# Moving two table builds beside the first MLP, 45 modulation columns into the sparse attention, and the first SwiGLU layer into seven-product blocks

## What is computed

```python
def first_block(...):             # one layer
    z = rms_norm(h, g_mix) @ w_in # q, k, v of sparse attention, an RNN, cross attention, gates
    y = gm0 * nsa_mixer(...) + gm1 * (gelu(g_rnn) * rg_lru(...)) + gm2 * cross_attention(...)
    h = h + y @ w_o
    h = h + square(relu(rms_norm(h, g_mlp) @ w_up)) @ w_down     # "the MLP", 1024 -> 4096 -> 1024
    return rms_norm(h, g_final)

def second_block(x, c, ...):      # two layers
    for l in range(2):
        mod = (silu(c) @ mod_w[l] + mod_b[l]).reshape(bsz, 3, 3, 1024)   # scale, shift, gain
        x = post_add(x, swiglu(pre(x, 0), ffn_w_in[l, 0], ffn_w_out[l, 0]), 0, 0.5)
        x = post_add(x, token_mixer(pre(x, 1), ...), 1, 1.0)   # state-space model and attention
        x = post_add(x, swiglu(pre(x, 2), ffn_w_in[l, 1], ffn_w_out[l, 1]), 2, 0.5)
```

## Time and profile before

| | |
|---|---|
| median of 3 runs | 3378.67 us (3377.63 to 3381.85) |
| the profiled execution, its own time | 3385.66 us |
| its span in the profile | 3383.9 us |
| PE busy | 3317.5 us, 98% |
| DVE, ACT, POOL busy | 62%, 43%, 13% |
| mean DMA rate | 118 GB/s |

### The profile page before, as it was taken

The page is one execution under the profiler, slowest core; times in us unless marked ns, Lnnn a source line. Parts: engine busy times, 40 slices in busy tenths (PEclk is TensorE's granted clock), DMA queues, the critical chain, the costliest instruction groups (busy, mean ns, idle before and its releaser), DMA issues.

```text
span 3383.9 us, 45115 instructions
## 1 busy us (share of the span) xinstructions
PE 3317.5 (98%) x18265; PEld 2709.1 (80%) x18273; DVE 2099.3 (62%) x3034; ACT 1439.4 (43%) x2316; POOL 427.6 (13%) x321
## 2 busy tenths in 40 slices
PE   9999999999999999999999999999999999999998
PEld 6755477688888888888768899979998875879998
DVE  5555566578687644565334777777777533367775
ACT  3365465442323332233443454445444245245543
POOL 0100012122232001022002100020001210220001
PEclk9999999999999999999999999999999999999999
DMA  5311543254655234213122132222323331222232
GB/s 195 138 55 60 184 180 142 107 192 180 251 215 197 98 126 153 87 64 136 69 83 98 64 108 98 100 88 94 107 107 110 115 106 44 101 74 100 95 106 75
DMA packets 83711, 398.01 MB, mean 118 GB/s; under 512 B 9136, under 2 KB 20016, under 8 KB 53296
## 3 DMA queue, kind: packets, MB, share of 16 engines
q1 hardware_dynamic: 71088, 370.41, 30.5%
q10 hardware_dynamic: 12416, 24.71, 2.0%
HBM read 374.12 MB, written 20.97 MB: 117 GB/s over the span
## 4 chain that ended last, share of the span: by engine, by line
PE 89%; DVE 6%; ACT 2%; issue 2%; POOL 1%; DMA 0%; SPq 0%; ACTq 0%; DVEq 0%; POOLq 0%
PE pb L817 13%; PE pb L819 13%; PE pb L818 13%; PE pb L1324 6%; PE pb L1323 6%; PE pb L1322 6%; PE pb L1363 3%; PE pb L1364 3%; PE pb L1365 3%; PE pb L718 2%; PE pb L785 2%; PE pb L786 2%; PE pb L1019 1%; PE pb L793 1%; PE pb L720 1%
## 5 line engine op out<-in xcount | busy, mean ns | idle before, releaser
L2453 DVE TENSOR_TENSOR wl<-w,wh 128x2048 fp32r<-128x2048 f32 (+2 forms) x179 | 390.4, 2181 | 439.6 <-ACT wh L1587 439.0
L817 PE MATMUL pb<-XH,wh 128*128 128x512 f32 (+2 forms) x1528 | 611.4, 400 | 2.3 <-DVE wl L2453 1.6
L819 PE MATMUL pb<-XH,wl 128*128 128x512 f32 (+2 forms) x1528 | 597.0, 391 | 0.0
L818 PE MATMUL pb<-XL,wh 128*128 128x512 f32 (+2 forms) x1528 | 596.7, 391 | 0.0
L1587 ACT ACTIVATE wh<-w 128x2048 fp32r<-128x2048 f32 (+2 forms) x179 | 309.6, 1729 | 178.0 <-PE pb L819 88.0
L817 PEld LDWEIGHTS pb<-XH,wh 128*128 128x128 f32 (+2 forms) x1528 | 286.1, 187 | 70.7 <-issue 8.2
L818 PEld LDWEIGHTS pb<-XL,wh 128*128 128x128 f32 (+2 forms) x1528 | 286.2, 187 | 64.1 <-issue 4.6
L819 PEld LDWEIGHTS pb<-XH,wl 128*128 128x128 f32 (+2 forms) x1528 | 285.7, 187 | 63.3
L1983 ACT ACTIVATE wh<-w 128x1024 fp32r<-128x1024 f32 x228 | 191.8, 842 | 91.1 <-DVE w L3012 75.5
L2997 DVE TENSOR_TENSOR wl<-w,wh 128x1024 fp32r<-128x1024 f32 x228 | 217.0, 953 | 13.8 <-ACT wh L1983 13.6
L2440 DVE CUSTOM_DVE_ANT_0 mreg<-mreg,pr 128x1024 f32<-128x1024 f32 x144 | 200.3, 1407 | 37.7 <-DMA mreg<-in_mod_w 37.4
(11 more groups left out here) (650 smaller groups left out, 7531.0 us busy)
## 6 DMA issues: line engine op xcount, KB each, us to landing
mreg<-in_mod_w SPq DMA_DIRECT2D x144, 512.0 KB, 3.5
w<-in_f_wide SPq DMA_DIRECT2D x57, 1024.0 KB, 4.8
w<-in_f_piece SPq DMA_DIRECT2D x48, 512.0 KB, 3.2
w<-in_f_in SPq DMA_DIRECT2D x22, 1024.0 KB, 4.8
w<-in_w_up SPq DMA_DIRECT2D x16, 1024.0 KB, 5.7
w<-in_w_dn SPq DMA_DIRECT2D x16, 1024.0 KB, 5.7
w<-in_m_g SPq DMA_DIRECT2D x16, 1024.0 KB, 4.8
w<-in_f_out SPq DMA_DIRECT2D x16, 768.0 KB, 4.2
```

The lines of the kernel that those rows point to most:

```text
L817: mm(dst, hi[:, cs], xh[:, k, :], start=k == 0, stop=False)
L818: mm(dst, hi[:, cs], xl[:, k, :], start=False, stop=False)
L819: x = mm(dst, lo[:, cs], xh[:, k, :], start=False, stop=fin)
L2453: tt(low[:, 0:s.cols], wslots[b % 3][:, 0:s.cols], h[:, 0:s.cols].bitcast(F32), ALU.subtract).then_inc(*DV.up(("lo", b), ("w_free", b)))
```

## The change

It does four things. All four SwiGLU layers use seven-product blocks, so the plain path is gone. Both table builds run beside the MLP: build 1 and then build 0, each padded to 66 steps, three steps a tile for the first 12 of the 64 tiles and two from there on; both layers' tables are stored to DRAM and loaded back at the end of layers 0 and 2. DVE's order inside a build is changed (the pieces `answers` before `lags`), with a second buffer for the turned weights, and both builds share one work space; build 0 waits for build 1's table store. And the modulation columns are spread anew: two for a block in the projections k, c, q (8 more loads), 21 in the rows half (after each third step) and all 8 of 8 steps in the keys half (64 in place of 48), one in place of two for a block of the MLP, where 12 are left of 57.

```diff
-        self.two_columns = name == "o" or name == ("m", 2) or name[0] in ("up", "dn")
+        self.two_columns = name in ("k", "c", "q", "o") or name == ("m", 2)
 for _n in range(64):
-    NSA_ROWS += [("s", _n)] + [("j", 0)] * (_n % 8 in (1, 4, 6)) + [("c", 0)] * (_n == 57) + [("y", 0)] * (_n == 59)
+    NSA_ROWS += [("s", _n)] + [("m", 0)] * (_n % 3 == 2) + [("j", 0)] * (_n % 8 in (1, 4, 6)) + [("c", 0)] * (_n == 57) + [("y", 0)] * (_n == 59)
...
-    NSA_KEYS += [("m", 0)] * (1 <= _j <= 6) + [("h", 0)] * (_n == 45)
+    NSA_KEYS += [("m", 0)] + [("h", 0)] * (_n == 45)
-WIDE_FFN = (1, 2, 3)
+WIDE_FFN = (0, 1, 2, 3)
-BUILD_A, BUILD_K, BUILD_B, BUILD_T = 16, 33, 34, 45
-BUILD_STORE = 59
+BUILD_A, BUILD_B, BUILD_K, BUILD_T = 18, 32, 43, 49
+BUILD_STORE, BUILD_END = 60, 66
+def some_steps(steps, tile):
+    for _ in range(3 if tile < 12 else 2):
+        next(steps, None)
...
                 if s.name == "qx":
-                    ahead(s.b[0] + 4)
-                    for n in range(48):
+                    for n in range(5):
+                        ahead(s.b[0] + n)
+                        for _ in range(4):
+                            mod()
+                    for n in range(1 + 64):
                         mod()
...
             def mlp():
-                extra = ssm_build(1)
+                extra, tile = itertools.chain(padded(ssm_build(1)), padded(ssm_build(0))), itertools.count()
...
             def ffn(l, f):
-                extra = ssm_build(0) if i == 0 else iter(())
...
+                run(st_of[("in", i, 0)], XH, XL, xw(r))
+                third_block(i)
+                for what, n in WIDE_STEPS:
+                    (wide_block if what == "i" else wide_piece)(i, n)
...
                 if s.name == ("in", 0, 0) and g == 0:
-                    act.wait_ge(tables_stored, 16)
+                    act.wait_ge(tables_stored, 32)
...
+                    if f == 0 and j == 0:
+                        act.wait_ge(*at("wide_done", i))
+                        act.dma_start(BIG[:, 12288:16384], ssm_turns[l]).then_inc(tables_landed, 16)
...
-                if nxt[1] == 2 or nxt == (1, 0):
+                if nxt[1] != 1:
                     t_sums(2 * nxt[0] + nxt[1] // 2, mc)
...
+                if l == 0:
+                    dve.wait_ge(tables_stored, 16)
...
                 for ft in range(4):
-                    if ft > 0:
-                        dve.wait_ge(*at("w_turn", l, ft - 1))
+                    m = (wt, wt_other)[ft % 2]
+                    if ft > 1:
+                        dve.wait_ge(*at("w_turn", l, ft - 2))
```

More of the change, by code:

```diff
@@ L161, with padded @@
 SSM_LOADS = [("si", 0), ("si", 1), "v", ("so", 0), ("si", 2), ("si", 3), ("so", 1), ("so", 2), ("so", 3)]
-BUILD_A, BUILD_K, BUILD_B, BUILD_T = 16, 33, 34, 45
-BUILD_STORE = 59
+BUILD_A, BUILD_B, BUILD_K, BUILD_T = 18, 32, 43, 49
+BUILD_STORE, BUILD_END = 60, 66
+def padded(steps):
+    n = 0
+    for _ in steps:
+        n += 1
+        yield
+    assert n <= BUILD_END
+    while n < BUILD_END:
+        n += 1
+        yield
+def some_steps(steps, tile):
+    for _ in range(3 if tile < 12 else 2):
+        next(steps, None)
 def plan(A, ssm_in, ssm_out):
@@ L1213, in mlp @@
             def mlp():
-                extra = ssm_build(1)
+                extra, tile = itertools.chain(padded(ssm_build(1)), padded(ssm_build(0))), itertools.count()
                 pairs = pairs_after("final", "sq")
                 def after():
-                    next(extra, None)
+                    some_steps(extra, next(tile))
                 def after_both():
-                    next(extra, None)
+                    after()
                     pairs()
@@ L1268, in ffn @@
                 i = 2 * l + f
-                extra = ssm_build(0) if i == 0 else iter(())
[L1270 to L1289, removed]
+                run(st_of[("in", i, 0)], XH, XL, xw(r))
+                third_block(i)
+                for what, n in WIDE_STEPS:
+                    (wide_block if what == "i" else wide_piece)(i, n)
+                pe.wait_ge(*at("gu", i, 20))
+                pe.wait_ge(*at("y_piece", i, 15, 1))
+                run(st_of[("out", i, 2)], HH, HL, hw(i, 2), pairs_after(r, "y_sq") if r != (1, 2) else None)
                 if r == (1, 2):
@@ L2007, in wide_first @@
             def wide_first(i):
-                r, before = (i // 2, 2 * (i % 2)), (i // 2, 1) if i % 2 else (i // 2 - 1, 2)
+                r, before = (i // 2, 2 * (i % 2)), ("final", (0, 1), (0, 2), (1, 1))[i]
                 s = st_of[("in", i, 0)]
@@ new lines, in ffn, with y_out @@
+                wide_first(i)
+                for j in WIDE_J:
+                    wide_cycle(i, j)
+                act.wait_ge(*at("gu", i, 21))
+                wide_high(i, 21)
+                def y_out(j, o, bank):
+                    if j == 7 and f == 0:
+                        hi_half(st_of[("u", l)], 1, 0)
+                    (last_square if r == (1, 2) else y_square)(r, j, at("y_new", i, j))
+                    if f == 0 and j == 0:
+                        act.wait_ge(*at("wide_done", i))
+                        act.dma_start(BIG[:, 12288:16384], ssm_turns[l]).then_inc(tables_landed, 16)
@@ L2235, in ffn @@
+                run(st_of[("out", i, 2)], y_out)
                 if r == (1, 2):
@@ L3161, in ssm_build @@
                 n = 0
-                w = [build_work[l][0][:, 32 * i:32 * i + 32] for i in range(12)]
+                w = [build_work[:, 32 * i:32 * i + 32] for i in range(12)]
                 def pw(i):
-                    a, b = build_work[l]
-                    return a[:, 384 + 32 * i:416 + 32 * i] if i < 4 else b[:, 32 * i - 128:32 * i - 96]
+                    return build_work[:, 384 + 32 * i:416 + 32 * i]
                 ar, dt, th, q, T_, em, rr, s1, s2, c1, t, d2 = w
@@ L3699, in ffn @@
                 i = 2 * l + f
-                for q, nk in enumerate((8, 8, 6) if i not in WIDE_FFN else ()):
-                    for j in range(nk):
-                        h_low((i, q), j, tmps[j % 4])
                 if r == (1, 2):
```

224 lines of the change are left out of this document (83 added, 141 removed).

## The result

The changed kernel takes 3469.18 us (median of 4 runs, 3468.01 to 3469.53) against 3378.67 us before, the median of its three fast runs (a fourth, slow one took 5915.41 us and is left out). The ratio is 1.0265, 95% interval 1.0245 to 1.0285: slower by 2.65%, far outside the forecast of 3369 to 3401 us. The profiled execution has a span of 3466.2 us, 82.3 more than before. (The medians are 90.5 us apart.

What follows compares the result with a forecast made beforehand. The prediction took PE, busy for 98% of the span, as the bound. Its terms, -22.3 + 7.3 + 6 + 3.5 + 12 + 2 = +8.5 us on the median of 3378.7, gave 3387 us, range 3369 to 3401 us.

Steps and rivals of the forecast that it cites:

- Layer 0: Layer 0 stage: seven-product blocks and build 0's PE work leaving bring it to layer 2's time, -22.3 us.
- rows half: Rows half: 21 added columns mostly fall into waits but cost where DVE has a backlog, +3.5 us.
- projections: Projections: 8 loads and 7 columns fit DVE's gaps of 3.5 to 4.7 us in every tile, 0 us.
- DVE at the start of the MLP: MLP's first stretch: 60 us of DVE work in 43.7 us makes PE wait, +6 us, bounds 0 and 17.
- walking the queue: Start of the MLP: `lo` of the fourth block some 2.5 us late, of the first down block 3.5.
- Build 0 in the rest of the MLP: MLP: build 0's four turns add PE work, 9.4 us, less a 2.1 us wait that goes away: +7.3 us.
- DVE catches up at two steps a tile: MLP after the first blocks: at two steps a tile DVE works off its backlog; no separate size.
- Columns in the keys half: Keys half: 64 columns, not 48, make a period of eight steps 19.0 us or more, +12 us, bounds 5 and 16.
- Start of the RNN: RNN start: DVE 9 to 10 us late from the keys half delays the second block's `lo`, +2 us, bounds 0 and 4.
- The first: Keys half: the 64 columns are hidden, MLP backlog and rows half cost half; -10 us, 3369 us, chance 0.16.
- second: No change that can be told: MLP backlog 0 to 2, keys half 5 to 8; 3377 us, chance 0.20.
- The third: MLP: DVE cannot work while POOL has the shared port; +15.5 or +20 us, 3394 to 3399 us, chance 0.14.

Runs made afterwards that it cites:

- The even pace: Changed kernel with both builds spread evenly over the MLP's 64 tiles, two steps a tile, three in every eighth: 3459.13 us (ratio to before 1.0238).

## Why the prediction was wrong

**Layer 0, rows half, projections: right.** -25.2, +3.4 and +0.3 against -22.3, +3.5 and 0. Two remarks on how exact that is. Of the 25.2 us some 3.4 are clock: in layer 0 PE worked for 6.8 us at the granted clock of 0.50 before, and not at all after. And the +3.4 of the rows half is partly luck: it is the difference of two single executions, and the rows half with its link took 131.7 to 136.4 us in three profiles without the 21 columns and 135.2 to 140.8 in twelve with them (means 133.3 and 138.0).

**DVE at the start of the MLP.** The amount was right: I had 60 us of DVE work, and DVE was busy for 63.3. Of the backlog of 17 us I let PE see 6, because "walking the queue" I followed only `lo`, and wrote of the next two blocks that "nothing is lost there". For `lo` it was right: PE waits 2.57 us before the fourth block (at 815.50), where I had 2.5. The step that failed is this one: PE's order has a second kind of instruction that needs DVE, the turns, and with three steps a tile the first of them (step 22) falls on the last tile of this very stretch. A turn waits for the build's newest work, so it sees the whole backlog: 14.37 us, and +24.1 in the stretch. The even pace took away 24.0 us there, and one tile more of distance another 8.7 and 8.1 us of the MLP in two arrangements.

**Build 0 in the rest of the MLP.** I had its turns only, +7.3 with the old wait of 2.1 us gone (PE's idle time in that stretch was 1.8: 50.30 less 48.52). The stretches from the second on grew by 32.8 us: 9.4 of turns (less the one that falls into the first stretch), some 16 of new waits and the low clock behind these. "DVE catches up at two steps a tile" was an average. DVE needs 306 us of work in 413 in the better arrangements, and the build's long pieces are bursts before fixed places: at 939.48 PE waits 4.23 us for a `lo` that stands behind 11.7 us of table doubling and a column without a gap (from 923.43 on), at 1038.44 3.49 us for build 0's first turn.

Not all of the new waits begin with DVE, and no term of the prediction had this. ACT issues the build's stores itself, and with `answers` before `lags` a large store now comes right before the eight small ones of line 2188:

```profile
905.08 0.33 ACTq L2182 DMA_DIRECT2D ssm_out<-BIG  x1
905.45 12.43 ACTq L2188 DMA_DIRECT2D ssm_out<-BIG  x8
917.98 0.60 ACT L1944 ACTIVATE tmps<-pb 128x512 f32<-128x512 f32 x1 [12.31 <-issue]
```

The eight took 4.9 us to issue in the kernel before. Here ACT stands for 12.31 us, PE waits 2.71 us for it at 918.63, and DVE, which waits 14.14 us for ACT's `hi`, comes to the table doubling above that much later. No run separates this from DVE's own load, so how much of the 27.7 us below is ACT's stays open, and so does why the issue takes longer here.

The columns add 0.5 to 0.9 us each in the MLP. In all arrangements tried the two builds cost the MLP 27.7 us or more, even with no column beside them, and layer 0 gives back 23 to 25: that alone makes the change no gain.

**Columns in the keys half.** Right in mechanism, place and sign; the term mis-sized is the pace. I took 2.3 us a column from the earlier trace rows and got 19.0 us for a period of eight steps. With eight columns in a row the loads land after 3.9 us (median), not 3.3, a column takes 2.6 to 2.8 us, and a period is 21.3 us long (PE's first and last wait of this kind end at 337.82 and 444.27 us, five periods apart). That is 4.2 over the 17.09 of before, five times 4.2 is 21: the 21.6 measured. The run without loads shows that DVE's own time has no part in it. Why the landing takes longer stays open; bursts to both buffers are closer together than before, but I did not separate the two.

**Start of the RNN.** Two errors. DVE was 17.4 us late, not 9 to 10 (the same pace), which made the first wait 8.64 us. And I wrote "SP is held by the same ticks, but two RNN blocks are loaded", and stopped there. The change issues `1 + 64` loads, so that SP is two columns ahead of DVE where it was one. In the RNN SP alternates a column load and a weight load; a column load waits for DVE's instruction two before it, so with a lead of two each weight load waits for the newest column instruction, a whole tile pair (12 to 15 us) later than before; the last of them cost 10.48 us. It shows in a single constant of the diff. That wait goes with the constant (0.55 us with one load less) and not with the late start (10.52 us with 48 columns in the keys half, where DVE is on time).

**The clock** was in no term. PE's granted clock was 1.00 in the keys half, the RNN and all but the last stretch of the MLP before, and 0.87 to 0.98 after. Where PE sets the pace this is time of its own: half of the busy time at the low clock is 12 us more than before in the MLP (30.7 us at the low clock against 6.8) and 4 in the RNN and merges (8.0 against 0). In the keys half, where DVE sets the period, I take it to cost nothing extra; no run shows this by itself.

**The rivals.** The first and second are refuted. The third, slower through the port that DVE shares with POOL, had the right sign but isn't the mechanism. The Trainium skill ("SBUF — State Buffer", section "SBUF: two separate sides") has the loser blocked for the whole instruction; here POOL was busy for 26.8 of the first stretch's 67.8 us. Of DVE's 87 instructions of 32 columns there, 64 took under 0.2 us and 8 took 0.8 to 1.3. All 8 overlap an instruction of POOL in time, but 11 others do so too and took 0.17 to 0.48 us. So the lengthening exists, but it is not the whole of POOL's busy time, and its size was in my estimate already: DVE's 63.3 us are near the 60.

**No version beat the kernel before.** The best three that compute the whole result are within 3411 to 3414 us, 1% above it.

## What to carry to other kernels

A backlog is seen first by the instruction with the closest tie to the late engine, so walk the waiting engine's whole order, not only its commonest wait. Where an issuing queue interleaves two streams, a constant that makes one stream run further ahead puts the other behind the newest consumer; check the lead at the border of stages. A pace read where a resource is now and then idle is a lower bound for what it does back to back.

## What the runs showed of the hardware

- A wait of PE of 6.3 us was followed by 5.6 us of work at 1.2 GHz, one of 15.0 us by 4.2 us; in the keys half waits of 1.9 to 3.4 us were each followed by a low clock in the records, those of 0.6 and 1.1 us not. Neither was one of 1.6 us in layer 2, nor one of 2.7 us in the MLP (918.63), so the length of the wait alone does not decide it.
- 512 KB loads through two buffers landed after 3.3 us (median) with six in eight steps and 3.9 us with eight.
- Eight small stores took ACT 12.43 us to issue right behind a larger one, and 4.9 us without it; ACT did nothing else meanwhile.
